# Three branch-A gate units in the third attention phase, the last four conditioning units after the output projection, and an FFN entry in another order

## What is computed

```python
shift1, scale1, gate1, shift2, scale2, gate2 = split(silu(c) @ w_ada + b_ada, 6)
h = modulate(rmsnorm(x, norm1_g), shift1, scale1)
gq, gk, gv, gr, glr, aq, ak, av, ga, gb = split(h @ w_in)
y_a = (rmsnorm(gla(gq, gk, gv, glr)) * silu(gr)) @ w_branch_a
y_b = (three groups of dilated window attention, joined by their denominators) @ w_branch_b
x = x + gate1 * ((sigmoid(ga) * y_a + sigmoid(gb) * y_b) @ w_out)
h2 = modulate(rmsnorm(x, norm2_g), shift2, scale2)
a, b = split(h2 @ w_up)
x = x + gate2 * ((silu(causal_conv3(a)) * b) @ w_down)
return rmsnorm(x) and the new states and caches
```

## Time and profile before

| | us |
|---|---|
| median of 3 runs | 1378.79 |
| lowest, highest | 1378.55, 1380.31 |
| the profiled execution | 1376.58 |
| its span, first to last instruction | 1374.9 |

### The profile page before, as it was taken

One profiled execution on the slowest core, in us unless ns is written; L12 is line 12 of the kernel. 1 busy time (PEld: TensorE's weight loads), 2 busy tenths in 40 slices (PEclk: granted clock), 3 DMA queues, 4 the chain that ended last, 5 costly groups with the idle time before them and its releaser, 6 DMA issues. The chain is left out here.

```text
span 1374.9 us, 23268 instructions
## 1 busy us (share of the span) xinstructions
PE 1247.2 (91%) x9753; PEld 1152.7 (84%) x9753; DVE 611.2 (44%) x958; ACT 484.9 (35%) x770; POOL 107.4 (8%) x193
## 2 busy tenths in 40 slices
PE   4599999999788999999988789997899999999997
PEld 3389998988677998888876568997799999999996
DVE  1622134454331344234444826654766565652332
ACT  2572243344433443244242215423533333322212
POOL 1000000001301000010112011100000000010000
PEclk9699999999899999999988679998899999999998
DMA  8536442323965646655656658833333333336771
GB/s 262 171 123 194 144 142 96 99 78 103 336 231 165 235 170 231 212 197 200 225 180 224 223 154 283 284 128 92 93 92 92 92 92 90 84 111 221 237 236 62
DMA packets 165377, 229.84 MB, mean 167 GB/s; under 512 B 7316, under 2 KB 147982, under 8 KB 163868
## 3 DMA queue, kind: packets, MB, share of 16 engines
q1 hardware_dynamic: 148532, 123.76, 29.4%
q10 hardware_dynamic: 1424, 54.52, 11.0%
q0 software_dynamic: 15344, 50.45, 10.7%
HBM read 202.96 MB, written 80.26 MB: 206 GB/s over the span
## 5 line engine op out<-in xcount | busy, mean ns | idle before, releaser
L362 PE MATMUL ps<-actH,whi 128*128 128x260 f32 x2064 | 446.7, 298 | 26.9 <-DVE actL L575 20.4
L362 PE MATMUL ps<-actH,wlo 128*128 128x260 f32 x2064 | 423.8, 288 | 0.0
L362 PE MATMUL ps<-actL,whi 128*128 128x260 f32 x2064 | 423.8, 288 | 0.0
L362 PEld LDWEIGHTS ps<-actH,whi 128*128 128x128 f32 x2064 | 327.1, 194 | 70.4 <-issue 55.1
L362 PEld LDWEIGHTS ps<-actL,whi 128*128 128x128 f32 x2064 | 327.5, 194 | 0.0
L362 PEld LDWEIGHTS ps<-actH,wlo 128*128 128x128 f32 x2064 | 326.8, 194 | 0.0
L346 DVE TENSOR_TENSOR wlo<-wraw,whi 128x512 fp32r<-128x512 f32 (+3 forms) x95 | 141.1, 1498 | 187.5 <-ACT whi L333 186.8
L333 ACT ACTIVATE whi<-wraw 128x512 fp32r<-128x512 f32 (+3 forms) x95 | 119.6, 1275 | 133.4 <-PE ps L362 92.9
L411 ACT ACTIVATE arena<-ps 128x520 f32<-128x520 f32 x76 | 45.5, 601 | 214.3 <-PE ps L362 214.0
L362 PE MATMUL ps<-gH,whi 128*128 128x260 f32 x352 | 71.1, 283 | 0.0
L362 PE MATMUL ps<-gH,wlo 128*128 128x260 f32 x352 | 70.8, 282 | 0.0
(11 more groups left out here) (306 smaller groups left out, 1467.9 us busy)
## 6 DMA issues: line engine op xcount, KB each, us to landing
wraw<-in_w_in SPq DMA_DIRECT2D x38, 1024.0 KB, 5.5
out_win_s<-in_cache_win ACTq DMA_DIRECT2D x16, 2046.0 KB
wraw<-in_w_ada SPq DMA_DIRECT2D x24, 1024.0 KB, 5.5
wraw<-in_w_up SPq DMA_DIRECT2D x44, 512.0 KB, 4.9
out_win_s<-in_cache_win ACTq DMA_DIRECT2D x8, 2044.0 KB
raw_gates<-arena SPq DMA_DIRECT2D x24, 260.0 KB, 5.3
arena<-raw_gates POOLq DMA_DIRECT2D x24, 260.0 KB, 4.4
wraw<-in_w_down SPq DMA_DIRECT2D x16, 384.0 KB, 3.4
```

The costliest lines, as they stand in the source:

```text
L362: last = pe.matmul(ps[:, 2 * (n % 2) + a, 0:HT], wt, X[:, k0 + j, a * HT:a * HT + HT], start=begin and j == 0 and wt is hi and X is H, sto ...
```

## The change

Three things change. The three ga units of att0 go to att2, alternating with gb: att0 has 6 units and not 9, att2 has 7 and not 4, so att0 has 24 places and not 36, att2 has 56 and not 32. With the units go three DRAM copies of caches and six spilled tiles. The number of steps is unchanged. Second, `ada` units 20 to 23 leave the stream. SP loads them (4 MB) into free parts of the arena once the mix is complete, and they are multiplied after the last `wo` unit, around the norm; DVE's Newton step (`refine_dve`) stands behind them. Third, the FFN's modulation is written out anew: the samples of all eight slices first, at once, the prompt with one scalar_tensor_tensor for each slice on DVE and one activation with bias on ACT, and the low part with one scalar_tensor_tensor. The first `up` unit takes slice after slice for both its tiles.

```diff
@@ -100,10 +101,10 @@
         ada(8 + u)
 
     add("aq0 gr aq0 gr ak0 gr ak0 gr av0 ga av0", "gla")
-    add("aq1 aq1 ga ak1 ga ak1 av1 ga av1", "att0")
+    add("aq1 aq1 ak1 ak1 av1 av1", "att0")
     add("aq2 aq2 ak2 ak2 av2 av2", "att1")
-    add("gb gb gb gb", "att2")
-    late = list(range(16, 23))
+    add("ga gb ga gb ga gb gb", "att2")
+    late = list(range(16, N_TAIL))
     for kind, src, n in (("bb", "w_branch_b", 2), ("ba", "w_branch_a", 4), ("wo", "w_out", 4)):
         for u in range(n):
...
@@ -112,7 +113,6 @@
                 cols(kind, w[src], 256 * u, 2)
             if late:
                 ada(late.pop(0))
-    ada(23)
 
     for u in range(KF):
...
@@ -488,15 +488,20 @@
 
         def ada_pe(pe, a):
 
-            u = ADA[a]
-            pe.wait_ge(w_dma[u % 2], U[u]["arrived"])
+            if a >= N_TAIL:
+                pe.wait_ge(s("ada_tail_in"), 16 * (N_ADA - N_TAIL))
+                wt = tail_slot[a - N_TAIL]
+            else:
+                u = ADA[a]
+                pe.wait_ge(w_dma[u % 2], U[u]["arrived"])
+                wt = wraw[:, u % 2, :]
             if a >= 1:
                 pe.wait_ge(ada_tok, a)
             for half in range(2):
                 for j in range(4):
                     k = 4 * half + j
                     last = pe.matmul(ps[QC * j:QC * j + QC, 7, 0:2 * P], scP[:, k, :],
-                                     wraw[:, u % 2, 2 * k * P:2 * (k + 1) * P], start=half == 0, stop=half == 1,
+                                     wt[:, 2 * k * P:2 * (k + 1) * P], start=half == 0, stop=half == 1,
                                      tile_position=(0, QC * j))
             last.then_inc(ada_done, 1)
...
@@ -556,6 +561,8 @@
             dve.wait_ge(s("sq_summed"), i + 1)
             dve.tensor_scalar(halves(tmp["v"]), ps[:, 4:6, 0:HT], 1.0 / D, EPS, ALU.mult, ALU.add)\
                .then_inc(s("ms_ready"), 1)
+
+        def refine_dve(dve, i, tmp):
             dve.wait_ge(s("rs_ready"), i + 1)
             dch.link(dve, newton(dve, tmp["v"], tmp["y"], tmp["t"], tmp["r"]))
...
@@ -586,6 +593,43 @@
                 if k >= 1:
                     low(k - 1)
             low(KD - 1)
+
+        def modulate_ffn_dve(dve, X, tmp):
+
+            g = vec[:, V_N2:V_N2 + KD].unsqueeze(2).to_broadcast([P, KD, NC])
+            shift, scale = 3 * KD, 4 * KD
+            dch.link(dve, dve.scalar_tensor_tensor(tmp["A"], mod[:, scale:scale + KD, :], 1.0, g, ALU.add, ALU.mult))
+            hs = tmp["hs"]
+            dch.link(dve, dve.tensor_tensor(hs, X[:, :, TP:T], tmp["r"][:, TP:T].unsqueeze(1).to_broadcast([P, KD, NS]),
+                                            ALU.mult))
+            dch.link(dve, dve.tensor_tensor(hs, hs, tmp["A"][:, :, 1:NC], ALU.mult))
+            dve.tensor_tensor(hs, hs, mod[:, shift:shift + KD, 1:NC], ALU.add).then_inc(s("h_ready"), 1)
+
+            def low(k):
+                dve.wait_ge(s("h_hi"), KD + 2 + k)
+                dve.scalar_tensor_tensor(actL[:, k, 0:TP], tmp["hf"][:, k % 2, 0:TP], mod[:, shift + k, 0:1],
+                                         actH[:, k, 0:TP].bitcast(F32), ALU.add, ALU.subtract).then_inc(s("h_split"), 1)
+
+            for k in range(KD):
+                if k >= 2:
+                    dve.wait_ge(s("h_split"), KD + k - 1)
+                dve.scalar_tensor_tensor(tmp["hf"][:, k % 2, 0:TP], X[:, k, 0:TP], tmp["A"][:, k, 0:1],
+                                         tmp["r"][:, 0:TP], ALU.mult, ALU.mult).then_inc(s("h_normed"), 1)
+                if k == 0:
+                    dve.wait_ge(s("h_hi"), KD + 1)
+                    dve.tensor_tensor(actL[:, :, TP:T], hs, actH[:, :, TP:T].bitcast(F32), ALU.subtract)
+                else:
+                    low(k - 1)
+            low(KD - 1)
+
+        def modulate_ffn_act(act, tmp):
+
+            act.wait_ge(s("h_ready"), KD + 1)
+            act.activation(actH[:, :, TP:T], tmp["hs"], ACT.Copy).then_inc(s("h_hi"), 1)
+            for k in range(KD):
+                act.wait_ge(s("h_normed"), KD + k + 1)
+                act.activation(actH[:, k, 0:TP], tmp["hf"][:, k % 2, 0:TP], ACT.Identity, bias=mod[:, 3 * KD + k, 0:1])\
+                   .then_inc(s("h_hi"), 1)
 
         def modulate_act(act, i, tmp, shift):
 
...
         ada4 = at(30200, 2, 2 * P)
         xT = at(FX, KD, T)
-        n2 = dict(norm_temps(0), A=at(4160, KD, NC))
+        n2 = dict(norm_temps(0), A=at(4160, KD, NC), hs=at(4240, KD, NS))
         G = {k: units(k) for k in ("bb", "ba", "wo", "up", "dn")}
 
         RAW = list(range(KD)) + [q + k * KD for q in range(KD) for k in (1, 2)]
...
-        def late_ada_dve(dve, a):
-            if a is not None:
-                ada_dve(dve, a, ada4)
-                if a > 16:
-                    ada_turn_dve(dve, a - 1)
-                if a == len(ADA) - 1:
-                    ada_turn_dve(dve, a)
+        tail_slot = [at(o, UW) for o in (8320, 8320 + UW, 16640, 16640 + UW)]
+        LATE = G["bb"] + G["ba"] + G["wo"]
+
+        def late_ada_pe(pe, u):
+            j = LATE.index(u)
+            if 16 + j < N_TAIL:
+                ada_pe(pe, 16 + j)
+            if 1 <= j <= N_TAIL - 16:
+                ada_turn_pe(pe, 15 + j, ada4)
+
+        def late_ada_dve(dve, u):
+            j = LATE.index(u)
+            if 16 + j < N_TAIL:
+                ada_dve(dve, 16 + j, ada4)
+            if 1 <= j <= N_TAIL - 16:
+                ada_turn_dve(dve, 15 + j)
 
         with nc.Block() as block:
             @block.sync
             def _(sp):
-                issue_all(sp, G["bb"][0] + 3, G["up"][0] + 2)
+                issue_all(sp, G["bb"][0] + 3, G["wo"][2] + 1)
+                sp.wait_ge(s("mixed"), KD)
+                for a in range(N_TAIL, N_ADA):
+                    src = w["w_ada"][:, 2 * P * a:2 * P * a + 2 * P].rearrange("(k p) n -> p k n", p=P)
+                    sp.dma_start(tail_slot[a - N_TAIL].rearrange("p (k n) -> p k n", k=KD), src).then_inc(s("ada_tail_in"), 16)
+                issue_all(sp, G["wo"][2] + 1, G["up"][0] + 2)
 
             @block.gpsimd
             def _(pool):
...
                         residual_dve(dve, n, 2 * j + m, 2 * KD)
                         square_dve(dve, 1, 2 * j + m - 1, n2)
-                    late_ada_dve(dve, ada_after(u))
+                    late_ada_dve(dve, u)
+                ada_dve(dve, N_TAIL, ada4)
                 square_dve(dve, 1, KD - 1, n2)
-                late_ada_dve(dve, 23)
                 rstd_dve(dve, 1, n2)
+                ada_turn_dve(dve, N_TAIL)
+                for a in range(N_TAIL + 1, N_ADA):
+                    ada_dve(dve, a, ada4)
+                    ada_turn_dve(dve, a)
+                refine_dve(dve, 1, n2)
 
             @block.tensor
             def _(pe):
                 for u in G["bb"]:
                     multiply(pe, u, b2H, b2L)
-                    late_ada_pe(pe, ada_after(u))
+                    late_ada_pe(pe, u)
                 for j, u in enumerate(G["ba"]):
                     multiply(pe, u, a2H, a2L, arriving=(s("a2_lo"), 0) if j == 0 else None)
-                    late_ada_pe(pe, ada_after(u))
+                    late_ada_pe(pe, u)
                 for j, u in enumerate(G["wo"]):
                     multiply(pe, u, actH, actL, arriving=(s("mix_lo"), 0) if j == 0 else None)
-                    late_ada_pe(pe, ada_after(u))
-                late_ada_pe(pe, 23)
+                    late_ada_pe(pe, u)
+                ada_pe(pe, N_TAIL)
                 norm_pe(pe, 1, n2)
+                ada_turn_pe(pe, N_TAIL, ada4)
+                for a in range(N_TAIL + 1, N_ADA):
+                    ada_pe(pe, a)
+                    ada_turn_pe(pe, a, ada4)
 
 
         abuf = at(FT, 2, T + 2)
...
                             pe.wait_ge(tile_read["act" if m == 0 else "dve"], (FA if m == 0 else FD) + d - 1 + 2 * i)
                         for k in range(KD):
-                            if first and d == 0 and m == 0:
-                                pe.wait_ge(s("h_split"), KD + k + 1)
                             last = three_pass(pe, n, (v0 + d) % 2, [KD * m + k], actH, actL, k0=k, begin=k == 0,
...
                     pe.transpose(ps[0:NS + 2, 6 + d, 0:P], abuf[:, d, TP:T + 2], ident).then_inc(s("tail_T"), 1)
 
-                unit(0, 0, True)
+                def first_unit():
+                    pe.wait_ge(lo_ready, v0 + 1)
+                    for n in (t0, t0 + 1):
+                        pe.wait_ge(tile_read[owner[n - 2]], freed[n - 2])
+                    for k in range(KD):
+                        pe.wait_ge(s("h_split"), KD + k + 1)
+                        for m in range(2):
+                            last = three_pass(pe, t0 + m, v0 % 2, [KD * m + k], actH, actL, k0=k, begin=k == 0,
+                                              end=k == KD - 1)
+                            if k == KD - 1:
+                                last.then_inc(pass_done, 1)
+
+                first_unit()
```

(4 more changed lines are left out.)

14 lines of the change are left out of this document (2 added, 12 removed).

## The result

The changed kernel takes **1402.82 us** (median of 4 runs, 1401.74 to 1408.18) against 1379.55 for the kernel before (4 runs, 1378.55 to 1382.28): a ratio of 1.0173, with a 95% interval of 1.0143 to 1.0204. I had forecast 1374.2, with a range up to 1386. The prediction was wrong in its sign, and the time lies outside its range. The profiled execution of the changed kernel has a span of 1400.1 us, 25.2 more than before.

A forecast was written before the change was run, and what follows sets the result against it. PE, busy 91% of the span, was taken as the bound. att0 and att1 -24.6, att2 +21.4, `bb` to `wo` -4.4, norm and first `up` unit +3.0: -4.6, so 1374.2 us median; case range 1367 to 1381, 8-in-10 range 1360 to 1386.

The forecast's parts named there:

- The join: In att2, steps 24 to 32: DVE sets the pace, 7.3 us more PE work vanishes; 35.5 us after 37.0, -1.5.
- my own sign of being wrong: Stated beforehand: the forecast is wrong if, among other signs, the join grows with the work put in it.
- Att2 ahead of the joins: To att2's fourth sample: +19.1 us of work, waits falling from 8.7 to 7.2, better clock giving 3.5: +14.1.
- Behind the joins: End of att2: 7 eighths become 13, +8.8 us; better clock against an uncovered spill landing, a further +1.8.
- Att0 and att1: Three units leave att0, -35.2 us; steps standing closer give some back: -24.6 in all (-31 to -13).
- (a): att0's flips: PE arrives 5.9 us earlier at the skewed bias; a later copy takes back 3.5: +2.4 (0 to +5.9).
- (b): att0: transposed sample rows directly precede the scores, exposing ACT's 1.02 us eviction, a half-size second and hand-overs: +1.9 us.
- (c): att0: seven pairs of attention steps stand together, two with a softmax still out: +2.2 us for both and small ones.
- The entry: Norm +7.2 us (late conditioning units chained at low clock), first `up` unit -4.2: together +3.0 (-3 to +5).
- B: Rival: PE's clock stays low in the join, making it slower: 1386 us; chance 0.15.
- C: Rival: waits move from att2 to att0, for keys (+8) and bias (+5.9): 1379 to 1383 us; chance 0.15.
- A: Rival: att0's crowding costs little, join clock holds, conditioning chain at full clock (-5): 1359 us; chance 0.25.

The follow-up runs named there:

- before_copies_out: The kernel before, without the four 2 MB cache copies of att2 (part of the window outputs not written): 1377.8 us, ratio 0.9953 to 1.0005.
- copies_out: The changed kernel without the seven 2 MB cache copies of att2 (part of the window outputs not written): 1379.5 us, ratio 0.997 to 1.0008.
- ffn_only: The changed kernel with the unit lists of the kernel before, so the reworked FFN entry alone: 1373.6 us, ratio 0.9919 to 0.9967.
- att0_copies_out: As copies_out, and also without the six cache copies of att0: 1375.6 us, ratio 0.9923 to 0.9984.

## Why the prediction was wrong, point by point

**The join, -1.5 forecast, +10.3 measured: the step that failed.** I argued that DVE's own work sets the cadence of a join (31.0 busy us of 37.0), so that more filler for PE would vanish in it. That holds only while DVE's inputs are there. I priced the added units in eighths of PE work alone. I knew that each unit issues a copy, weights and two spills, had used the 263 GB/s of that very stretch for the `ada` loads, and had let a copy slow the bias loads in att0; in att2, where the DMA share was already 0.75, the highest of all rows, I gave the three units' transfers no term (but for the landing of the last spill) and no rival. From the first join to the fourth it is +10.4 (24.4 to 34.8), and +2.4 where neither kernel has copies in att2 (before_copies_out to copies_out, 24.5 to 26.9): near the argument, which had put 8 us of transfers at nothing. A join that grows with the work put in it was my own sign of being wrong. It came, though it was the transfers of that work, and not its products, that made it grow.

**Att2 ahead of the joins, +14.1 forecast, +18.0 measured.** The same miss, at the key store: in that pair of kernels without copies it is +12.7 (74.4 to 87.1). Behind the joins it is +11.5 there, as much as with the copies, for a forecast of +8.8; that miss is not the copies', and what makes it stays open. For all of att2 the pair gives +26.6, the change +39.5, the forecast was +21.4. So the missing term was 12.9 us, the 17.1 that copies cost att2 in the changed kernel less the 4.2 that they had cost before, and other terms were 5.2 short. In totals the pair differs by +1.7 us (1377.8 to 1379.5), no difference clear of the noise: where no copies crowd att2 the loss is gone, but the gain of 4.6 isn't there either.

**Att0 and att1, -24.6 forecast, -17.4 measured.** The terms mis-sized are (a), (b) and (c). For the bias I took +2.4 where the wait grew by 4.3, from 4.3 to 8.6: PE came 7.0 us earlier, not 5.9, and the loads landed 2.7 us sooner (10.0 us after their issue, 12.6 before), not 3.5. The copy that I held against the bias loads was of 0.5 MB, not 2 MB, as are all three copies that begin in att0's first three units; I had read the size of most of the group and not of those. SP's next 1 MB of weights (420.62 before, 435.99 after) left the loads' time as well, so which of the two slowed them is not shown. Steps together: I counted two exposed pairs and 1.9 us of exposed sample rows, together with the small term 4.7; the four waits at L1380 grew by 5.2 (6.2 against 1.0), and two new waits at L1368 make 3.8, one of them behind the eviction of the sample rows, as (b) had it. The lower clock cost 2.5 us (busy 125.4 for 158.1 - 35.2 = 122.9), forecast 2. The run with eighths shows what placing at quarters costs in all, with its clock: 12 us, and att0 and att1 are then at -27.7.

**The entry, +3.0 forecast for norm and first unit, +0.4 measured**, and `bb` to `wo` -3.0 for -4.4. The mechanism came as described. PE's late conditioning units run at half clock, each 985.47 - 982.03 = 3.44 us in a chain, forecast 3.4; Exp ends at 981.63 and the Newton step starts at 989.10. After, PE in that chain:

```profile
982.03 1.94 PE L503 MATMUL ps<-arena,scP 128*32 128x256 f32 x16
984.51 1.02 PE L514 MATMUL ps<-cst,arena 128*128 128x9 f32 x4 [0.55 <-DVE arena L522]
985.47 1.94 PE L503 MATMUL ps<-arena,scP 128*32 128x256 f32 x16
```

The norm's own matmuls and the first turn came before the clock fell at 978.4, 4.2 us behind the last product; I had put the fall ahead of them, as in the kernel before. In two other kernels with the same code it fell later: 8.5 us behind the last product in ffn_only and 11.7 in att0_copies_out (in five more 4.4 to 4.7), and the norm takes 21.1, 18.6 and 17.2 us accordingly. At full clock a unit of the chain takes 953.30 - 951.14 = 2.16 us (ffn_only):

```profile
951.14 1.07 PE L503 MATMUL ps<-arena,scP 128*32 128x256 f32 x16
...
953.30 1.07 PE L503 MATMUL ps<-arena,scP 128*32 128x256 f32 x16
```

The first `up` unit took 13.3 us, forecast 14.2.

**The rivals.** B had the right sign for another reason: the clock in the joins is 0.82, above the 0.72 of before, and 0.89 behind them. A clock that stays low was not the cause. C's longer wait for the bias came in most of its size (+4.3 for +5.9), and that for the keys didn't (5.7 us of DVE's waits in att0, 6.7 before). A fell; its chain counts as -5 in the list and as -4.4 in the sum, a slip that changes nothing. The case that came, loads that arrive late in the joins, was not among them; it should have been, since a rule that I had quoted says it. The Trainium skill, "DMA: Bandwidth & Descriptors", section "Issuing engines are not separate DMA queues": transfers of ScalarE, SyncE and GpSimd run on the same engines and interleave. The trace agrees: loads of POOL and SP landed 18 us after their issue beside a copy of ACT's.

## What to carry to other kernels

When filler work is moved, its transfers move with it: list each DMA that the moved unit issues, and look at the DMA share and the landings of the stretch that receives it, before counting in the time of the engine that is the bound. Transfers that nobody waits for belong where the DMA share is low and loads are asked for well ahead; here eight 2 MB copies beside the `up` units cost nothing, and the wrong one in the joins cost 6 us. Filler is worth as much as its spacing: with a third fewer units, steps placed twice as finely gave back 12 us of that phase. The same edit with all units there cost it 7, and here too by a transfer: it put a 2 MB store beside loads that are waited for.

## What the runs showed of the hardware

- With the queues full (DMA share 1.03, 353 GB/s over 26 us), a load issued behind a 2 MB copy from DRAM to DRAM landed 20.2 us after its issue (762.73 to 782.94) and 14.5 without the copy (761.35 to 775.88); the difference is about the copy's own 5.2 us of the 16 engines. Weights, value loads and spills in flight with it landed 5.1 to 5.5 us sooner without it.
- The flips could start 9.9 to 12.6 us after the issue of 2 MB of bias loads in eight kernels, and 19.0 and 19.7 us after it in the two where 1 MB of weights and a 2 MB store were issued within 0.6 us of them.
- The `up` loop took 174 GB/s in place of 90 with no change in PE's pace.
- In one and the same piece of code behind the last `wo` product, the granted clock fell 4.2, 8.5 or 11.7 us later in three kernels, which made the norm 21.1, 18.6 or 17.2 us long. What decided it stays open: the code ahead was the same for 100 us.
- The code before the first product of the stream took 56.2 to 62.1 us in the profiles of the twelve kernels. That too stays open; a difference of two single profiles has to be read with such a stretch in mind.
